# One gate projection per layer moved from the branch loop into the attention stage

## The reference

```python
h = rmsnorm(x, norm1_g[layer]) * (1 + sc1) + sh1
proj = h @ w_in_l                 # Fourier | conv | pool | q | k | v | 4 gates of width 1024
attn = latent_attention(q, concatenate([k, kc]), concatenate([v, vc]))
...
merged = sum(jax.nn.sigmoid(proj[..., OFF_G + i * D_MODEL:OFF_G + (i + 1) * D_MODEL]) * br
             for i, br in enumerate((f, cv, pl, at)))      # br: each branch @ its own matrix
x = x + g1 * (merged @ lp['w_out'])
```

## Time and profile before

| what | us |
|---|---|
| median of the timed runs (3) | 2173.99 |
| lowest and highest of them | 2171.55, 2177.05 |
| the profiled execution | 2172.3 |
| its span, first to last instruction | 2170.5 |
| attention of layer 0 (first score to last values) | 157.13 to 205.32 |
| attention of layer 1 | 961.67 to 992.45 |

### The profile page before, as it was taken

How to read it: one execution, slowest core, us unless ns; L and a number is a source line. 1 busy time by engine, 2 the same in 40 slices (tenths; PEclk the granted TensorE clock), 3 DMA queues, 4 the chain that set the end, 5 groups by cost and what they waited for, 6 DMA issues and landing times.

```text
span 2170.5 us, 28873 instructions
## 1 busy us (share of the span) xinstructions
PE 2085.4 (96%) x10178; PEld 1721.6 (79%) x10178; DVE 1769.9 (82%) x2279; ACT 1185.4 (55%) x1442; POOL 42.5 (2%) x84
## 2 busy tenths in 40 slices
PE   8989999997999999789999999999999999999997
PEld 6765888876888887658997888888888888888886
DVE  7786877887676676777866989899898989899895
ACT  3416233324333332435466777777777777777774
POOL 0000000000000000000000000000000000000000
PEclk9999999998999999899999999999999999999999
DMA  8510234453444443313555999989898999989893
GB/s 325 194 35 1 97 112 136 176 202 117 174 154 155 174 152 119 124 66 101 186 198 211 395 354 357 372 326 380 337 384 334 373 356 354 372 326 390 330 376 120
DMA packets 77289, 512.44 MB, mean 236 GB/s; under 512 B 8738, under 2 KB 9890, under 8 KB 22820
## 3 DMA queue, kind: packets, MB, share of 16 engines
q1 hardware_dynamic: 65700, 469.59, 57.2%
q0 software_dynamic: 11520, 41.95, 5.5%
HBM read 510.46 MB, written 1.05 MB: 236 GB/s over the span
## 4 chain that ended last, share of the span: by engine, by line
PE 84%; DVE 10%; issue 2%; ACT 2%; DMA 1%; SPq 0%; DVEq 0%; ACTq 0%; POOL 0%; POOLq 0%
PE bank L893 9%; PE bank L891 9%; PE bank L892 9%; PE bank L912 5%; PE bank L914 5%; PE bank L913 5%; PE bank L652 4%; PE bank L654 4%; PE bank L653 4%; PE bank L820 2%; DVE tile_low L1443 2%; PE bank L822 2%; PE bank L821 2%; PE bank L805 2%; PE bank L795 2%
## 5 line engine op out<-in xcount | busy, mean ns | idle before, releaser
L1019 ACT ACTIVATE down_high<-W 128x1024 fp32r<-128x1024 f32 x224 | 237.0, 1063 | 120.9 <-PE bank L914 120.8
L1394 DVE TENSOR_TENSOR up_b_low<-W,up_b_high 128x2048 fp32r<-128x2048 f32 x112 | 256.5, 2290 | 51.2 <-ACT up_b_high L1012 51.1
L1401 DVE TENSOR_TENSOR down_low<-W,down_high 128x1024 fp32r<-128x1024 f32 x224 | 270.0, 1222 | 16.9 <-ACT down_high L1019 3.5
L1388 DVE TENSOR_TENSOR up_a_low<-W,up_a_high 128x2048 fp32r<-128x2048 f32 x112 | 255.8, 2284 | 0.2 <-ACT up_a_high L1006 0.2
L652 PE MATMUL bank<-h_high,tile_high 128*128 128x512 f32 (+1 forms) x704 | 238.1, 338 | 1.0 <-DVE tile_low L1443 1.0
L653 PE MATMUL bank<-h_low,tile_high 128*128 128x512 f32 (+1 forms) x704 | 236.4, 336 | 0.0
L654 PE MATMUL bank<-h_high,tile_low 128*128 128x512 f32 (+1 forms) x704 | 236.4, 336 | 0.0
L1006 ACT ACTIVATE up_a_high<-W 128x2048 fp32r<-128x2048 f32 x112 | 213.0, 1902 | 0.6 <-PE bank L893 0.6
L1012 ACT ACTIVATE up_b_high<-W 128x2048 fp32r<-128x2048 f32 x112 | 213.1, 1903 | 0.0
L912 PE MATMUL bank<-down_high,mact_high 128*128 128x512 f32 x448 | 183.0, 408 | 2.7 <-DVE down_low L1401 2.7
L914 PE MATMUL bank<-down_low,mact_high 128*128 128x512 f32 x448 | 175.5, 392 | 0.0
(11 more groups left out here) (274 smaller groups left out, 4316.3 us busy)
## 6 DMA issues: line engine op xcount, KB each, us to landing
W<-in_moe_up SPq DMA_DIRECT2D x224, 1024.0 KB, 6.8
W<-in_moe_down SPq DMA_DIRECT2D x112, 1024.0 KB, 6.6
W<-in_w_mod_later POOLq DMA_DIRECT2D x80, 512.0 KB, 3.7
W<-in_ffn SPq DMA_DIRECT2D x33, 1024.0 KB, 4.8
W<-in_attn_blocks SPq DMA_DIRECT2D x24, 1280.0 KB, 6.2
W<-in_attn_blocks SPq DMA_DIRECT2D x22, 1024.0 KB, 6.0
W<-in_attn_blocks SPq DMA_DIRECT2D x8, 1536.0 KB, 6.6
shift_tiles<-in_w_mod_first SPq DMA_DIRECT2D x8, 512.0 KB, 14.2
```

The lines of the kernel that those rows point to most:

```text
L1388: tt(al[u][:], raw_a[u].rearrange("p (k n) -> p k n", k=KD // 2), ah[u][:].bitcast(F32), ALU.subtract) \
L1394: tt(bl[u][:], raw_b[u].rearrange("p (k n) -> p k n", k=KD // 2), bh[u][:].bitcast(F32), ALU.subtract) \
L1401: tt(cl[:, h, :], raw_c[u][:, h * D:(h + 1) * D], ch[:, h, :].bitcast(F32), ALU.subtract) \
```

## The change

`gate00`, the first gate tile of each layer, leaves branch step 0. PE now makes it in the attention, in round p = 1, behind S2 and S3 and ahead of T0, all 24 matmuls in one piece. ACT copies it from PSUM into `sg` behind exp(4) and ahead of keep_turned(1), and takes the sigmoid in place from `sg` to `sg` in branch step 0, where it took it from PSUM before. DVE waits on a semaphore of its own (`early_gate`) for it. The order of the PSUM results has `gate00` behind S3; its bank is taken out of the round until S7 has got its bank, and banks are no longer counted off mod 8 but walked through.

```diff
+EARLY = [f"gate{BRANCH_ORDER[0]}{j}" for j in range(1)]
+def early_plan(layer):
+    return [(1, 0, k) for k in range(KD)]
+def early_end(layer, t):
+    return max(p for p, tile, _ in early_plan(layer) if tile == t)
 def psum_order(layer):
         order += [f"S{u}" for u in (2 * p, 2 * p + 1) if u < n]
         if p >= 4 and p % 2 == 0:
             order.append(f"V{p // 2 - 2}")
+        order += [EARLY[t] for at, t, k in early_plan(layer) if at == p and k == 0]
+        order += ["-" + EARLY[t] for t in range(1) if p == early_end(layer, t) + 2]
         order += [f"T{u}" for u in (2 * p - 3, 2 * p - 2) if 0 <= u < n]
-            order += [f"gate{i}{j}", f"branch{i}{j}"]
+            if f"gate{i}{j}" not in EARLY:
+                order.append(f"gate{i}{j}")
+            order.append(f"branch{i}{j}")
-        use = {}
+        uses, held, bank = [0] * 8, {}, 0
         for layer in range(DEPTH):
             for name in psum_order(layer):
-                use[layer, name] = (len(use) % 8, len(use) // 8)
+                if name[0] == "-":
+                    del held[name[1:]]
+                    continue
+                while bank in held.values():
+                    bank = (bank + 1) % 8
+                use[layer, name] = (bank, uses[bank])
+                uses[bank] += 1
+                if name in EARLY:
+                    held[name] = bank
+                bank = (bank + 1) % 8
PE:
+                def early_gate(t, k):
+                    tile = layer * len(TILES) + TILE_NO[EARLY[t]]
+                    r = tile % TILE_RING
+                    if k == 0:
+                        pe.wait_ge(S("tile_low_ready"), tile + 1)
+                        opened(layer, EARLY[t])
+                    b = banks[use[layer, EARLY[t]][0]]
+                    mm(b[:, 0:N], wh[:, r, k, :], hh[:, k, 0:N], start=k == 0, stop=False)
+                    mm(b[:, 0:N], wh[:, r, k, :], hl[:, k, 0:N], start=False, stop=False)
+                    last = mm(b[:, 0:N], wl[:, r, k, :], hh[:, k, 0:N], start=False, stop=k == KD - 1)
+                    if k == KD - 1:
+                        done(layer, EARLY[t], last)
+                    for at, t, k in early_plan(layer):
+                        if at == p:
+                            early_gate(t, k)
-                    project(f"gate{i}{j}")
+                    if f"gate{i}{j}" not in EARLY:
+                        project(f"gate{i}{j}")
ACT, in the attention:
+                    for t in range(len(EARLY)):
+                        if u == 2 * early_end(layer, t) + 2:
+                            act.wait_ge(S("conv_gated"), 2 * layer + 2)
+                            b = filled(act, layer, EARLY[t])
+                            fn(sg[:, t, 0:N], b[:, 0:N], ACT.Copy).then_inc(free(layer, EARLY[t]), 1)
ACT, in the branch steps:
-                    if step == 0:
-                        act.wait_ge(S("conv_gated"), 2 * layer + 2)
+                    if step < len(EARLY):
+                        read(act, layer, EARLY[step])
+                        fn(sg[:, step, 0:N], sg[:, step, 0:N], ACT.Sigmoid).then_inc(S("early_gate"), 1)
DVE:
-                    read(dve, layer, f"gate{i}{j}")
+                    if n < len(EARLY):
+                        dve.wait_ge(S("early_gate"), len(EARLY) * layer + n + 1)
+                    else:
+                        read(dve, layer, f"gate{i}{j}")
```

More of the change, by code:

```diff
@@ L304, in build @@
         seq = C("seq").rearrange("p (c t) -> p c t", c=2)
-        use = {}
+        use, uses_to = {}, []
+        uses, held, bank = [0] * 8, {}, 0
         for layer in range(DEPTH):
             for name in psum_order(layer):
-                use[layer, name] = (len(use) % 8, len(use) // 8)
-        uses_to = [len(psum_order(0)), len(use)]
+                if name[0] == "-":
[8 more added lines that the diff above has]
+                bank = (bank + 1) % 8
+            uses_to.append(list(uses))
         def filled(eng, layer, name):
@@ L578, in values @@
                     done(layer, f"V{v}", last)
+                N = T if layer == 0 else LAT
+                def early_gate(t, k):
[10 more added lines that the diff above has]
+                        done(layer, EARLY[t], last)
                 n = len(units)
@@ L778, in attention_half @@
                 for b in range(8):
-                    pe.wait_ge(S(f"bank_free{b}"), len(range(b, uses_to[layer], 8)))
+                    pe.wait_ge(S(f"bank_free{b}"), uses_to[layer][b])
             modulation()
@@ L1151, in attention_half @@
                             .then_inc(free(layer, "convnorm"), 1)
-                    if step == 0:
-                        act.wait_ge(S("conv_gated"), 2 * layer + 2)
[L1154 to L1157, removed]
+                    if step < len(EARLY):
+                        read(act, layer, EARLY[step])
+                        fn(sg[:, step, 0:N], sg[:, step, 0:N], ACT.Sigmoid).then_inc(S("early_gate"), 1)
+                    else:
+                        if step >= 2:
+                            read(act, layer, step_name(step - 2))
+                        b = filled(act, layer, f"gate{i}{j}")
+                        fn(sg[:, step % 2, 0:N], b[:, 0:N], ACT.Sigmoid).then_inc(free(layer, f"gate{i}{j}"), 1)
                     split(layer, TILE_NO[f"gate{i}{j}"] + TILE_RING)
```

## The result

The changed kernel takes 2169.4 us (median of 16 runs, 2167.2 to 2170.8), the kernel before 2172.9 (16 runs, 2169.0 to 2177.4). The ratio is 0.9982 with an interval of 0.9975 to 0.9989: 2.4 to 5.4 us faster, 3.9 at the ratio itself. (The medians themselves are 3.5 apart.) That is a real gain, and inside the 0.3% that I had taken for "no change that can be told".

The account below looks back on a forecast made before the run. PE was taken to set the pace (busy 96% of the span), with a 2.03 us hole near each attention's start. Gains of 2.2 (layer 0) and 2.4 (layer 1) sum to 4.6: 2174.0 - 4.6 = 2169.4 us, likeliest 2167.5 to 2171.5.

Parts of the forecast that it names:

- T0 3.4 later: Layer 0's attention start: gate fills some 2.1 us of PE's hole, so T0 moves from 161.15 to 164.56.
- V0 of layer 0 2.5 later: Layer 0's first values, after ACT's exponentials, new copy and keeps, move from 168.80 to 171.3.
- V0 of layer 1 0.45 later: Layer 1's attention: first values and the rest 0.45 us later, from a maximum 0.2 late and 0.28 of copy.
- The rounds behind keep their pitch: Layer 0's attention behind V0: same work on the same engines, PE nearly without a hole, so the delay stays 2.5.
- rival (b): Attention hides the whole gate, later rounds catching up the start's loss: gain 8.3 us, 2165.7; chance 0.13.
- The lost cover: Ahead of branch00: the moved gate had covered 0.91 us of waiting for W_low, which now comes out.
- The early sigmoid in layer 1: Layer 1's first branch steps: sigmoid ready early, DVE's product follows branch00, branch01 starts at 997.5 without its 0.78 wait.
- Layer gains: Gain at branch00 of layer 0, 2.2 us, and at branch01 of layer 1, 2.4 us; sum 4.6.
- The clock at the start of layer 0: Filling the hole keeps full clock for S4 and S5; a fall all the same takes 0.8 us off the gain.
- The bank: gate00's PSUM bank in the attention: seven results use the seven other banks before its release, so holding it costs nothing.
- Rival (c): Bank round one shorter, scores wait 0.53 more for each of 12 value sets: 6.4 lost, 1.8 slower, 2175.8; chance 0.05.
- Chances: Whole kernel: same 0.77, faster 0.17, slower 0.06, told apart from about 0.3%, 6.5 us; the forecast itself 0.58.

Follow-up runs that it names:

- round_later: The change with the early gate (copy and bank release too) one round later, behind S4 and S5; ratio to the kernel before 1.0006.
- w_low_first: The change, with DVE making W_low of the first branch matrix ahead of the last keep_values; 2167.8 us, ratio to the kernel before 0.9976.
- l1_only: The change in layer 1 alone, layer 0 with the old code; ratio to the kernel before 0.9991, 2.0 us faster.
- tail_pieces: Kernel before, with gate00 cut into three pieces around the attention's last values, no early gate or copy; ratio to the kernel before 0.9989.
- two_gates: w_low_first plus gate01 in pieces around the last values and the second branch split ahead of step 0; 2164.4 us, ratio to the kernel before 0.9965.

## Why the prediction was right

Predicted 2169.4, measured 2169.4; gain of 4.6 forecast, 3.9 by the ratio, 4.5 in the traces. That the time agrees to the tenth is luck: I subtracted 4.6 from the median of three runs of the kernel before, 2174.0, and sixteen runs put it at 2172.9; the medians are only 3.5 apart, and the two errors of 1.1 cancel. The mechanism stands on its own. Step by step:

- **The holes fill, the rest shifts.** T0 3.4 later: 3.46 (7.48 behind the first score instead of 4.02). V0 of layer 0 2.5 later: 2.55. V0 of layer 1 0.45 later: 0.53. The rounds behind keep their pitch: V0 to V7 is 35.50 before and 35.51 after, so rival (b) falls: the rounds catch up nothing. round_later shows the other side: the same gate off the hole gains nothing.
- **The lost cover.** 0.91 us in each layer: 0.90 and 0.90. w_low_first takes 0.79 and 0.86 of it away, and that reaches out0 and the router in full.
- **The early sigmoid in layer 1.** `branch01` 2.4 sooner: 2.33.
- **Layer gains** 2.2 and 2.4: 2.05 at branch00 and 1.94 at out0; 2.33 at branch01 and 2.54 at the router. Each layer alone gives its part.
- **The clock at the start of layer 0** is the one term that holds only in part. I took it that filling the hole saves the fall. Of the ten traces without the hole none shows a fall there; of the four with it three do (before, l1_only, round_later; not tail_pieces), and of the four with the same hole in layer 1 none. The 0.8 us belong to those executions in which the clock falls, not to all; without them the layer's gain at branch00 is 2.05 - 0.78 = 1.27.
- **The bank.** That holding it costs nothing was right, by more than I had argued. Rival (c) was wrong in its mechanism too: with a round of seven in earnest the 0.68 us wait comes, and is hidden by the keep on ACT that the values wait for. My step "S12 would too, 0.53 more each time" took a wait on PE for a delay of the chain.
- **Chances.** I put the bound for faster at 0.3%; the interval of the result ends at 0.25%. The class was "same", as given 0.77.

**What stays open.** When the clock falls behind a hole of 2 us. The hole and what PE does ahead of it in layer 0 are the same in traces that fall and in the one that does not. Also open is why the expert stage, the same code everywhere, takes 1006.1 to 1009.9 us; its 3.8 us of spread are as much as the gain, and no experiment here was made for it.

I took the hole behind S3 as given. Part of it is the table load for the exponentials, on an engine that had stood idle for 28.76 us (timeline of ACT in the kernel before, layer 0; layer 1 has the same):

```profile
158.30 1.28 ACT L1132 ACT_TABLE_LOAD   x1 [28.76 <-PE bank L557]
159.59 0.69 ACT L1132 ACTIVATE prob<-bank,stat 128x512 f32<-128x512 f32 x1
```

The first maximum starts at 158.26, and a later exponential starts 0.71 behind the start of its maximum (161.01 to 161.72); so the load holds up the first exponential by about 0.6 us, an estimate from these rows. Loading the table ahead of the first score was not tried; it would make the hole smaller in place of filling it.

## What to carry to other kernels

Find the engine that paces the stage, look for its holes, and move in work that has its inputs already; the gain is the hole, less what the work covered where it stood, and neither the amount moved nor the share of busy time says anything about it. Then ask what waited behind the moved work: here one DVE instruction in the wrong order cost half of what a hole brought. Before pulling work ahead in every step, follow it to the end of the loop: each step's own result comes a piece later, which counts in full where another engine takes over the pace, and the last step is left with a hole, behind which the clock can fall.

## What the runs showed of the hardware that I had not expected

The same hole of 2.03 us on TensorE was followed by the half clock (1.2 GHz) in three of four traces in layer 0 and in none of four in layer 1, with full clock granted just before in both. A hole of the same size, the 2.05 us ahead of the matmul of out0 that waits for the last merged part in layer 0, was followed by it in nine of twelve traces (not in l1_only, round_later and two_gates). It stands behind the mark out0, so the table does not show it; from that mark to the last matmul of the output projection are 41.3 us with the fall, in before (41.32) and with the change (41.30) alike, and 39.8 without it. A fall cost 0.8 us where short turns and scores ran under it (V0 11.67 against 10.89), 1.5 in that output projection and 1.6 where a gate did (l1_only, branch00 55.40 against 53.76). The Trainium skill describes the monitor's window as free-running ("TensorE: Matmul & The Clock Gate", What's actually happening); that the same instructions at one place fall in one trace and not in another agrees with it, and no run here tests it.
